# Early stage of a conditioned decoder trunk: five weight places by table, and section weights split by column halves

## The chip, the cores and the metric

The kernel runs on one core of a Trainium2 chip. The time is device microseconds (us) of one execution. The kernel before takes 1154.68 us, the median of three runs (1153.91 to 1155.73). In what follows PE is TensorE, DVE is VectorE, ACT is ScalarE, POOL is GpSimd and SP is SyncE, whose queue issues nearly all of the transfers (DMAs).

## The reference

One layer on 256 tokens of width 1024, all in fp32:

```
mod = silu(c) @ w_ada + b_ada                 # six vectors of 1024: shift, scale, gate, twice
h   = rms_norm(x) * (1 + scale_mix) + shift_mix
z   = h @ w_in                                # 1024 x 7168: sc_x | sc_B | sc_C | u | v | gate_A | gate_B
yA  = sc_B * causal_dwconv3(sc_C * sc_x)
yB  = gelu(u) * (tril(W_s) @ layer_norm(gelu(v)) * ... + b_s)   # ln_v_g is the weight of that norm
x   = x + gate_mix * ((sigmoid(gate_A)*yA + sigmoid(gate_B)*yB) @ w_out)
h   = rms_norm(x) * (1 + scale_ffn) + shift_ffn
x   = x + gate_ffn * moe(h)                   # top 4 of 32 experts, clamped SwiGLU, 12 MiB of weights each
out = rms_norm(x)
```

The spatial product W_s @ v mixes tokens and leaves the channels apart, so the norm's weight, which is one number for each channel, may be put on before the product or after it.

## The kernel before, in words

**Two parts.** The early stage (the adaptive modulation, the projection w_in and the mixer, w_out) reads 28 units of 2 MiB of weights. Then the router orders the experts, and the expert part reads 192 units of 2 MiB, six for each expert, through twelve places in SBUF. Both streams, and a few small tables, are issued one after another by SP, so a transfer whose place isn't free holds back all that are behind it.

**The early units.** The list `units` gives the order. Those called "ada" are slices of w_ada, those called "in" are half a section of w_in (1024 rows by 512 columns; sections are V, then SC_C, SC_X, SC_B, GATE_A, U, GATE_B for the left half of the channels, h = 0, and again for h = 1), and "out" are the halves of w_out. They land in the tile raw, a ring of three places (0, 1, 2), in order of their number. Two early ones go aside, to the tile spare and to slot 7 of the tile W. A unit may be loaded when the one three before it in the ring was used up.

**Split products.** A product in fp32 is made of three passes in a reduced format: ACT copies the weights into wh (`split_high`, L556), DVE subtracts to get wl (`split_low`, L743), and PE makes hh*wh, hl*wh and hh*wl (`product`, L1093). There are two pairs wh, wl in turns, so the weights of section j are split while PE works on section j-1, once it has finished with j-2. Before, each unit is split in two pieces by rows (k), so PE can finish nothing of a section until both pieces are there, and ACT can begin the next unit in that pair only when the whole section is done.

**A section.** PE makes a section in two halves of 256 columns (b = 0, 1), each 48 matmuls of 128x256. I number these halves m = 0 to 23. Behind PE, ACT and DVE take each half out of PSUM and do the convolution, the gates and so on, in the order of an explicit loop over h, section and b. In the same loop DVE splits the section after the next (at b = 1) and works through the adaptive weights of the later four vectors (`weigh`, L790 to L793): each ada unit is multiplied by silu(c) and added into `weighed`, which lies in spare, two passes of 128x2048 a unit, eight units in all. PE sums over the partitions afterwards (`sum_weighed`).

**Spatial product.** In front of the half U, b = 0 PE makes `spatial(2h)` into bank B6, behind U, b = 1 `spatial(2h+1)` into the same bank. The latter waits for `sp_used`: DVE must have taken the former out of B6.

**Going over to the experts.** The first expert units are loaded under waits written by hand: the first when `ada_summed` is 2 (in spare), the second when GATE_B of h = 1 is split, the third when the first half of w_out is split, the fourth when the last section half is done on PE, and so on.

## Time and profile before

| | |
|---|---|
| median of 3 runs | 1154.68 us (1153.91 to 1155.73) |
| profiled execution, span | 1151.8 us (the page gives no other time for it; 2.9 us below the median) |
| PE busy | 957.4 us (83%) |
| DVE, ACT busy | 357.2 us (31%), 243.4 us (21%) |
| moved by DMA | 467.30 MB, mean 406 GB/s |
| last section half on PE | 203.7 us |
| third expert unit issued | 198.23 us |

How to read it: shares are of the whole span, and say little of the first 250 us, where the work is different from the rest. The page's second part cuts the span in 40 slices of 28.8 us. Its first eight slices are the early stage and the router, the rest is the expert part.

### The profile page before, as it was taken

The numbers are of one execution on the slowest core, as the hardware profiler recorded it, in microseconds if no ns is written. First come the engines' busy times: TensorE is split into PE (matmuls) and PEld (weight loads), VectorE is DVE, ScalarE is ACT, GpSimd is POOL, SyncE is SP. The second block draws the span as 40 slices with busy tenths as digits, with TensorE's granted clock in tenths as the row PEclk, the third lists the DMA queues.
The fourth block names the chain that finished last, engine by engine and source line by source line (L and its number), as shares of the span: only waits on it lengthen the run. The fifth ranks groups of instructions, "written<-read, shape, count | busy, mean of one in ns | idle before, by whom it ended". The sixth has DMA issues, their size and how long they took to land.

```text
span 1151.8 us, 23787 instructions
## 1 busy us (share of the span) xinstructions
PE 957.4 (83%) x9707; PEld 505.7 (44%) x9708; DVE 357.2 (31%) x801; ACT 243.4 (21%) x365; POOL 8.6 (1%) x28
## 2 busy tenths in 40 slices
PE   7989999998986976987888888888876876876784
PEld 5789999743442321433333333443321322331331
DVE  3689796571221111212121121221211211211112
ACT  3435444530110110111111111110100100100112
POOL 0010000000000000000000000000000000000000
PEclk9989999999998998999998999999998998898997
DMA  9999788999999999999999999999999999999996
GB/s 358 377 340 357 293 311 318 412 400 428 427 425 427 426 426 427 426 426 425 425 426 427 427 426 426 427 426 427 426 426 426 427 426 427 427 426 426 427 424 273
DMA packets 62413, 467.30 MB, mean 406 GB/s; under 512 B 5180, under 2 KB 6516, under 8 KB 27572
## 3 DMA queue, kind: packets, MB, share of 16 engines
q1 hardware_dynamic: 62144, 466.65, 98.1%
q8 instruction: 19, 0.31, 0.1%
q10 hardware_dynamic: 244, 0.29, 0.1%
q14 instruction: 6, 0.05, 0.0%
HBM read 465.87 MB, written 1.05 MB: 405 GB/s over the span
## 4 chain that ended last, share of the span: by engine, by line
PE 42%; DMA 40%; SPq 8%; DVE 6%; issue 4%; ACT 1%; PEldq 0%; DVEq 0%; ACTq 0%
PE B L1405 22%; DMA trio<-in_w_down_dram 21%; DMA W<-in_w_down_dram 14%; PE B L1093 10%; SPq L411 4%; PE B L1424 3%; DMA W<-in_w_gate_up_dram 3%; SPq L413 3%; PE B L1414 2%; DVE wl L743 2%; DMA spare<-in_w_ada_dram 2%; PE B L1351 2%; PE B L1357 1%; DMA raw<-in_w_in_dram 1%; DVE spare L793 1%
## 5 line engine op out<-in xcount | busy, mean ns | idle before, releaser
L1405 PE MATMUL B<-W,trio 128*32 128x512 f32 (+1 forms) x4784 | 451.4, 522 | 85.6 <-DMA W<-in_w_gate_up_dram 77.3
L1405 PEld LDWEIGHTS B<-W,trio 128*32 128x32 f32 x4784 | 163.3, 112 | 347.7 <-issue 168.2
L661 ACT ACTIVATE EW<-EW 128x256 f32<-128x256 f32 x46 | 19.2, 416 | 683.1 <-DVE EW L1023 683.1
L1023 DVE TENSOR_SCALAR EW<-B 128x256 f32<-128x256 f32 x46 | 19.5, 425 | 463.9 <-PE B L1405 463.9
L1093 PE MATMUL B<-hh,wh 128*128 128x256 f32 x384 | 110.4, 288 | 4.2 <-DVE wl L743 4.2
L1093 PE MATMUL B<-hl,wh 128*128 128x256 f32 x384 | 109.8, 286 | 0.0
L1093 PE MATMUL B<-hh,wl 128*128 128x256 f32 x384 | 109.7, 286 | 0.0
L1414 PE MATMUL B<-b_gu,trio 128*32 128x512 f32 x368 | 50.4, 616 | 66.6 <-issue 55.2
L743 DVE TENSOR_TENSOR wl<-raw,wh 128x2048 fp32r<-128x2048 f32 (+1 forms) x36 | 73.3, 2074 | 18.2 <-ACT wh L556 17.7
L556 ACT ACTIVATE wh<-raw 128x2048 fp32r<-128x2048 f32 (+1 forms) x36 | 60.2, 1719 | 84.0 <-DMA raw<-in_w_in_dram 53.8
L1093 PEld LDWEIGHTS B<-hh,wh 128*128 128x128 f32 x384 | 74.9, 195 | 4.6 <-issue 4.0
L1093 PEld LDWEIGHTS B<-hl,wh 128*128 128x128 f32 x384 | 74.9, 195 | 0.0
L1093 PEld LDWEIGHTS B<-hh,wl 128*128 128x128 f32 x384 | 74.9, 195 | 0.0
L1424 PE MATMUL B<-EW,trio 32*128 32x256 f32 x752 | 67.1, 426 | 8.6 <-PE B L1424 7.8
L1038 DVE TENSOR_TENSOR EW<-B,trio 128x256 f32<-128x256 f32 x46 | 19.5, 425 | 150.4 <-PE B L1405 150.4
L661 ACT ACT_TABLE_LOAD x46 | 59.0, 1283 | 5.8 <-issue 5.0
L1405 PE MATMUL B<-trio 128*32 128x256 f32 x736 | 44.3, 380 | 12.2 <-DMA trio<-in_w_down_dram 12.2
L1351 PE MATMUL B<-HV,trio 128*32 128x256 f32 x752 | 53.7, 400 | 0.2 <-DVE trio L959 0.2
L1405 PE MATMUL B<-spare,trio 128*32 128x512 f32 x368 | 51.7, 678 | 0.0
L1424 PEld LDWEIGHTS B<-EW,trio 32*128 32x128 f32 x752 | 29.4, 182 | 47.7 <-PE B L1424 26.6
L1351 PEld LDWEIGHTS B<-HV,trio 128*32 128x32 f32 x752 | 30.2, 120 | 41.8 <-issue 35.6
L1414 PEld LDWEIGHTS B<-b_gu,trio 128*32 128x32 f32 x368 | 8.6, 107 | 87.8 <-issue 87.8
(245 smaller groups left out, 689.8 us busy)
## 6 DMA issues: line engine op xcount, KB each, us to landing
W<-in_w_gate_up_dram SPq DMA_DIRECT2D x112, 2048.0 KB, 35.2
W<-in_w_down_dram SPq DMA_DIRECT2D x48, 2048.0 KB, 38.4
spare<-in_w_gate_up_dram SPq DMA_DIRECT2D x16, 2048.0 KB, 28.6
trio<-in_w_down_dram SPq DMA_DIRECT2D x15, 2048.0 KB, 41.0
raw<-in_w_in_dram SPq DMA_DIRECT2D x12, 2048.0 KB, 9.5
raw<-in_w_ada_dram SPq DMA_DIRECT2D x9, 2048.0 KB, 9.6
raw<-in_w_in_dram SPq DMA_DIRECT2D x4, 1024.0 KB, 15.7
raw<-in_w_out_dram SPq DMA_DIRECT2D x2, 2048.0 KB, 8.9
```

What stands on the lines that cost most here:

```text
L411: sp.dma_start(unit_pair(u).rearrange("p g n -> p (g n)"), gu_v[e, j]).then_inc(s_unit[u % SLOTS], 16)
L413: sp.dma_start(unit_pair(u), dn_v[e, j - NQ]).then_inc(s_unit[u % SLOTS], 16)
L556: A(part_of(wh[j % 2], c, j), part_of(src, c, j), ACT.Copy).then_inc(split_h, 1)
L661: A(sg, gs, ACT.Sigmoid, scale=ALPHA).then_inc(sig_ready, 1)
L743: V.tensor_tensor(part_of(wl[j % 2], c, j), part_of(src, c, j), part_of(wh[j % 2], c, j).bitcast(f32), ALU.subtract).then_inc(split_l, 1)
L1023: V.tensor_scalar(halves(gs), paired(GU[:, 0:QC]), LIMIT, None, ALU.min).then_inc(gmin_ready, 1)
L1038: V.tensor_tensor(yw, Db[:, 0:QC], gfq, ALU.mult).then_inc(yw_ready, 1)
L1093: t = M(o, left[i], right[j], start=(k == 0 and n == 0), stop=(k == KT - 1 and n == 2))
L1351: t = M(Db[CAP * g:CAP * g + CAP, 0:QC], S[:, a, CAP * g:CAP * g + CAP], HV[:, a, g * QC:(g + 1) * QC], start=(a == 0), stop=(a == TA - 1))
L1405: t = M(o, src[:, k % KQ, CAP * (k // KQ):CAP * (k // KQ) + CAP], w, start=(first and k == 0), stop=(k == KT - 1))
L1414: M(GU[CAP * g:CAP * g + CAP, :], sel[:, g, :], b_gu[:, :], start=True, stop=False)
L1424: M(Yb[a][h][:, (g % 2) * QC:(g % 2) * QC + QC], SwT[rows_, a * P:(a + 1) * P], yw[rows_, :], start=False, stop=True, skip_group_check=Tru ...
```

## The change

- The ring is replaced by a table `homes` that gives each unit its order and one of five places: R0, R1, R2 in raw, the tile spare (which now takes SC_X of h = 0 too) and slot 7 of W (SC_B and GATE_B of h = 0 too). A unit may be loaded when the last one in the same place was used up.
- The section units are split by column halves: piece b holds the columns that half b of the section needs. Piece m + 3 is split in step m, on ACT and on DVE, so the split runs three halves ahead, and a piece waits only for the same half of the section two before.
- `weigh` of the eight units goes to steps m = 1, 4, 7, 8, 12, 14, 17, 19.
- The tables of the mixer (w_spatial, b_spatial, b_ada) are asked for after the ada unit (1, 1), those of the router after GATE_B of h = 0.
- ln_v_g is read as one column per 128 channels with the other small rows, and multiplied in when DVE takes the spatial product out of PSUM (two scalar_tensor_tensor of 128x256 in place of one add of 128x512). The broadcast of it to 128 partitions (512 KiB) and two multiplications of 128x1024 go.
- The first modulation is cut in two around the transposes of x, the router's helper steps (`fhT`, `spread`) move behind the products with w_out.
- The first expert unit now waits for GATE_B's split, the second for `ada_summed`, and the third, as before, for the split of the first half of w_out; but that is now made in two pieces at steps m = 22 and 23, where before the whole of it was made in step m = 21.

```diff
+    homes = [
+        (("ada", 0, 0), R0), (("ada", 0, 1), R1), (("in", V_, 0), R2), (("ada", 0, 2), ASIDE_SPARE), (("ada", 0, 3), ASIDE_M), (("in", V_, 1), R0),
+        (("in", SC_C, 0), R1), (("in", SC_X, 0), ASIDE_SPARE), (("in", SC_B, 0), ASIDE_M), (("ada", 1, 0), R2), (("in", GATE_A, 0), R0), (("ada", 1, 1), R1),
...
+        (("in", SC_B, 1), R2), (("ada", 2, 0), R0), (("in", GATE_A, 1), R1), (("ada", 2, 1), R0), (("ada", 2, 2), R0), (("in", U_, 1), R2),
+        (("in", GATE_B, 1), R1), (("ada", 2, 3), R0), (("out", 0, 0), R2), (("out", 0, 1), R0)]
+    WEIGH_AT = {1: (1, 0), 4: (1, 1), 7: (1, 2), 8: (1, 3), 12: (2, 0), 14: (2, 1), 17: (2, 2), 19: (2, 3)}
...
-            sp.wait_ge(ada_summed, NH)
-            load(0, 0)
             sp.wait_ge(split_l, pieces_before[-3])
+            load(0, 0)
+            sp.wait_ge(ada_summed, NH)
             load(1, 0)
             sp.wait_ge(split_l, pieces_before[-2])
             load(2, 0)
...
-                        if b == 1 and NS * h + n < NS * NH - 1:
-                            split_low(NH + NS * h + n + 2)
+                        m = 2 * (NS * h + n) + b
+                        if 1 <= m < HALVES - 3:
+                            piece_low(m + 3)
+                        if m >= HALVES - 2:
+                            split_low(NH + NS * NH, (b,))
...
+                        if m in WEIGH_AT:
+                            weigh(*WEIGH_AT[m])
...
-                            V.tensor_tensor(stmp.rearrange("p (t a n) -> p t a n", t=2, a=TA),
-                                            B[6][:, :].rearrange("p (t a n) -> p t a n", t=2, a=TA), bias, ALU.add).then_inc(sp_used, 1)
+                            for t in range(2):
+                                k = 4 * h + 2 * b + t
+                                ins = V.scalar_tensor_tensor(gated[:, t], spread_v[:, t], cols[:, 7 * KT + k:7 * KT + k + 1],
+                                                             bs_all[:, k:k + 1, :].broadcast_to([P, TA, P]), ALU.mult, ALU.add)
+                            ins.then_inc(sp_used, 1)
...
-                        if b == 0 and n < 3:
-                            weigh(1 + h, n + 1)
-                        if b == 0 and s == GATE_B and h + 1 < NH:
-                            weigh(2 + h, 0)
...
+                        half_ready(j, b)
                         for tt in range(2):
                             for k in range(KT):
-                                split_ready(j, k)
...
+                    if s == U_ and h == 1:
+                        sum_weighed(2)
```

On DVE, the steps ahead of the first use of the spatial product (bank B6). Before, from the third section's second half on (L743 is a split, L863 the use of B6, L867 what follows it):

```order
L854 TENSOR_TENSOR tmp<-tmp,B5 128x512
L858 TENSOR_TENSOR tmp<-tmp 128x512
L743 TENSOR_TENSOR wl1<-raw,wh1 128x2048 x2
L858 TENSOR_TENSOR tmp<-tmp 128x512
L863 TENSOR_TENSOR tmp<-B6,tmp 128x512
L867 TENSOR_TENSOR tmp<-tmp 128x512
```

And now (L759 is a piece of a split, L808 and L809 are weigh, L892 is the use of B6):

```order
L883 TENSOR_TENSOR tmp<-tmp 128x512
L759 TENSOR_TENSOR wl1<-W,wh1 128x8x256
L808 SCALAR_TENSOR_TENSOR spare<-raw,tmp,spare 128x2048
L809 SCALAR_TENSOR_TENSOR spare<-raw,tmp,spare 128x2048
L883 TENSOR_TENSOR tmp<-tmp 128x512
L759 TENSOR_TENSOR wl1<-W,wh1 128x8x256
L808 SCALAR_TENSOR_TENSOR spare<-raw,tmp,spare 128x2048
L809 SCALAR_TENSOR_TENSOR spare<-raw,tmp,spare 128x2048
L892 SCALAR_TENSOR_TENSOR tmp<-B6,cols,tmp 128x256 x2
L897 TENSOR_TENSOR tmp<-tmp 128x512
```

Two weigh steps, of the ada units (1, 2) and (1, 3), now stand close ahead of the use of B6, the second of them directly with a split piece ahead of it; before, neither stood between GATE_A and B6.

On SP, the early units behind the router's tables (the last row of which is given first). Before:

```order
L405 DMA EW<-in_b_down_dram 32x512 x4
L385 DMA raw<-in_w_ada_dram 128x2x2048
L385 DMA raw<-in_w_in_dram 128x8x512 x3
L385 DMA raw<-in_w_ada_dram 128x2x2048
L385 DMA raw<-in_w_in_dram 128x8x512
L385 DMA raw<-in_w_ada_dram 128x2x2048
L385 DMA raw<-in_w_in_dram 128x8x512
L385 DMA raw<-in_w_ada_dram 128x2x2048
L385 DMA raw<-in_w_in_dram 128x8x512
L385 DMA raw<-in_w_ada_dram 128x2x2048
L385 DMA raw<-in_w_in_dram 128x8x512 x2
L385 DMA raw<-in_w_out_dram 128x8x512 x2
```

And now:

```order
L408 DMA EW<-in_b_down_dram 32x512 x4
L390 DMA raw<-in_w_ada_dram 128x2x2048
L390 DMA raw<-in_w_in_dram 128x8x512
L390 DMA raw<-in_w_ada_dram 128x2x2048
L390 DMA raw<-in_w_in_dram 128x8x512 x2
L390 DMA raw<-in_w_ada_dram 128x2x2048
L390 DMA raw<-in_w_in_dram 128x8x512
L390 DMA raw<-in_w_ada_dram 128x2x2048 x2
L390 DMA raw<-in_w_in_dram 128x8x512 x2
L390 DMA raw<-in_w_ada_dram 128x2x2048
L390 DMA raw<-in_w_out_dram 128x8x512 x2
```

Before, behind the tables stand the ada units (1, 3) and (2, 0) to (2, 3); now (1, 2) and (1, 3), and then the same four, of which (2, 1) and (2, 2) stand together. By the table all four of h = 1 go to one place, R0. The ada unit (1, 3) is now the 17th unit, before it was the 14th.

## Rows read from the trace of the kernel before

**Rows 1.** Page, part 2: DMA share and rate in 40 slices
```profile
DMA  9999788999999999999999999999999999999996
GB/s 358 377 340 357 293 311 318 412 400 428 427 425 427 426 426 427 426 426 425 425 426 427 427 426 426 427 426 427 426 426 426 427 426 427 427 426 426 427 424 273
```

**Rows 2.** Windows: stretch, length, PE clock, DMA share, GB/s
```profile
195.00:198.00 3.00, 1.00 0.12 49
198.00:204.00 6.00, 1.00 0.82 294
204.00:255.00 51.00, 1.00 0.99 403
```

**Rows 3.** Timeline of SP: start, length of issue, third and thirteenth expert unit
```profile
198.23 0.33 SPq L411 DMA_DIRECT2D W<-in_w_gate_up_dram  x1
...
249.98 0.38 SPq L411 DMA_DIRECT2D spare<-in_w_gate_up_dram  x1
```

**Rows 4.** Line L1093 in 50 to 235 us: ns min/median/max, first and last start
```profile
L1093 PE MATMUL B<-hh,wh x384: 277/283/553, 51.6 to 203.5; 128*128 128x256 f32 x192
...
L1093 PE MATMUL B<-hh,wl x384: 278/283/415, 51.9 to 203.7; 128*128 128x256 f32 x192
```

**Rows 5.** Chain that ended last: start, length, what
```profile
119.51 0.89 PE B L1224 x8
120.41 57.59 PE B L1093 x480
178.00 0.99 PE B L1143 x8
```

**Rows 6.** Timeline of PE, first product of the third section
```profile
79.53 0.55 PE L1093 MATMUL B<-hh,wh 128*128 128x256 f32 x1 [3.82 <-DVE wl L743]
```

**Rows 7.** Windows, PE alone: busy, clock, DMA share, GB/s
```profile
76.00:79.50 3.50, 0.00 (x0) 0.85 0.55 158
79.50:85.30 5.80, 5.77 (x27) 0.50 1.08 365
```

**Rows 8.** Timeline of PE, column sums in the second half of V
```profile
38.28 0.96 PE L1131 MATMUL B<-stat,mod 128*128 128x1 f32 x8
```

**Rows 9.** DMA issues of 10.4 us: KB each, us to landing
```profile
W<-in_w_ada_dram SPq DMA_DIRECT2D x1, 2048.0 KB, 23.6
```

**Rows 10.** Windows: PE clock, DMA share, GB/s
```profile
2.00:42.50 40.50, 1.00 1.03 388
...
2.00:106.00 104.00, 0.97 0.99 362
```

**Rows 11.** Timeline of DVE, a section step and a weigh
```profile
81.50 0.68 DVE L844 TENSOR_TENSOR tmp<-tmp,B 128x512 f32<-128x512 f32 x1
82.22 0.35 DVE L849 TENSOR_SCALAR tmp<-tmp,cols 128x256 f32<-128x256 f32 x1
82.61 0.48 DVE L850 SCALAR_TENSOR_TENSOR tmp<-tmp,cols 128x255 f32<-128x255 f32 x1
...
85.07 2.35 DVE L792 SCALAR_TENSOR_TENSOR spare<-raw,tmp,spare 128x2048 f32<-128x2048 f32 x1
```

**Rows 12.** Timeline of DVE, a split and what follows it
```profile
89.85 2.29 DVE L743 TENSOR_TENSOR wl<-raw,wh 128x2048 fp32r<-128x2048 f32 x1
...
94.26 0.68 DVE L844 TENSOR_TENSOR tmp<-tmp,B 128x512 f32<-128x512 f32 x1
```

**Rows 13.** Timeline of ACT, a split and a copy out of PSUM
```profile
75.00 3.71 ACT L556 ACTIVATE wh<-raw 128x2048 fp32r<-128x2048 f32 x2 [6.39 <-DMA raw<-in_w_in_dram]
78.62 0.58 ACT L610 ACTIVATE tmp<-B 128x512 f32<-128x512 f32 x1
```

**Rows 14.** DMA issues of 87.4, 126.2 and 133.1 us, in that order
```profile
raw<-in_w_ada_dram SPq DMA_DIRECT2D x1, 2048.0 KB, 7.6
raw<-in_w_ada_dram SPq DMA_DIRECT2D x1, 2048.0 KB, 8.6
raw<-in_w_in_dram SPq DMA_DIRECT2D x1, 2048.0 KB, 8.0
```

**Rows 15.** Chain that ended last, in the first expert rounds
```profile
260.52 1.57 issue
...
263.16 6.87 PE B L1405 x64
...
276.96 2.08 issue
...
280.21 8.45 PE B L1405 x64
```

More of the change, by code:

```diff
@@ L76, in hybrid_trunk @@
     unit_no = {u: n for n, u in enumerate(units)}
+    in_order = [("in", V_, h) for h in range(NH)] + [("in", s, h) for h in range(NH) for s in SECTIONS] + [("out", 0, h) for h in range(NH)]
+    assert [units[n] for n in split_units] == in_order
     NU = len(units)
@@ L174, in hybrid_trunk @@
         id_row, more_row, unit_row, upto, passed, hit_round, round_row = [order_row(6 + i) for i in range(7)]
-        rank_col, id_col, more_col, owner, expert_col, place_rank = [stat[:, 51 + i:52 + i] for i in range(6)]
+        rank_col, id_col, more_col, owner, expert_col = [stat[:, 51 + i:52 + i] for i in range(5)]
         rounds = mod[0:1, 1, 0:6 * E + 1].bitcast(i32)
@@ L308, in act_bank, with home, in_section, product_done @@
             return act_order.index((h, s, b)) + 1
-        ASIDE = (3, 4)
-        aside_at = (spare[:, :], slot(7))
-        def place(n):
-            return n if n < ASIDE[0] else n - len(ASIDE)
+        def home(n):
+            return homes[n][1]
         def raw_slot(n):
-            if n in ASIDE:
-                return aside_at[ASIDE.index(n)]
-            return raw[:, (place(n) % RING) * UW:(place(n) % RING + 1) * UW]
+            if home(n) == ASIDE_SPARE:
+                return spare[:, :]
+            if home(n) == ASIDE_M:
+                return slot(7)
+            return raw[:, home(n) * UW:(home(n) + 1) * UW]
         def landed(n):
-            if n in ASIDE:
-                return s_aside[ASIDE.index(n)], 16
-            return s_slot[place(n) % RING], 16 * (place(n) // RING + 1)
-        def product_done(eng, j):
+            return s_slot[home(n)], 16 * len([m for m in range(n + 1) if home(m) == home(n)])
+        def in_section(j):
+            return NH <= j < NH + NH * NS
+        def product_done(eng, j, c):
             if j == 0:
@@ L356, in _ @@
             for n, (kind, s, h) in enumerate(units):
-                if n not in ASIDE and place(n) >= RING:
-                    m = next(o for o in range(n) if o not in ASIDE and place(o) == place(n) - RING)
+                before_it = [m for m in range(n) if home(m) == home(n)]
+                if before_it:
+                    m = before_it[-1]
                     if m in ada_units:
@@ L796, in weigh, with piece_low @@
                     dve.nop().then_inc(weighed_ready, 1)
-            split_low(2)
-            weigh(1, 0)
-            split_low(3)
+            def piece_low(t):
+                split_low(NH + t // 2, (t % 2,))
+            piece_low(0)
+            piece_low(1)
             dve.wait_ge(v_gelu, TA * NH)
@@ L1103, in _, with modulation @@
             keep_warm(WARM_FIRST, B[5])
-            pe.wait_ge(s_rows, 64)
-            TR(B[6][:, 0:7 * KT], rows, ident[0:7 * KT, 0:7 * KT]).then_inc(rowsT_done, 1)
-            def modulation(part, g):
+            pe.wait_ge(s_rows, 80)
+            TR(B[6][:, 0:8 * KT], rows, ident[0:8 * KT, 0:8 * KT]).then_inc(rowsT_done, 1)
+            def modulation(part, g, ks=range(KT)):
                 if part + g == 0:
@@ L1113, in modulation @@
                 n = unit_no[("ada", 0, 2 * part + g)]
-                if part == 0 and g == 1:
+                if part == 0 and g == 1 and ks[0] == 0:
                     pe.wait_ge(s_ada_top, 16)
@@ L1118, in modulation @@
                 w = raw_slot(n).rearrange("p (k n) -> p k n", k=KT)
-                for k in range(KT):
+                for k in ks:
                     j = k % 4
-                    if part == 0 and g == 1 and k == 4:
-                        arrived(n)
                     t = M(first_bank(part, g)[32 * j:32 * j + 32, :], cond[:, k, :], w[:, k, :], start=(k < 4), stop=(k >= 4))
-                t.then_inc(ada_used, 1)
+                if ks[-1] == KT - 1:
+                    t.then_inc(ada_used, 1)
             def turn_sums(part, g):
@@ L1146, in _ @@
             modulation(0, 0)
+            modulation(0, 1, range(0, 4))
             pe.wait_ge(xn_ready, TA)
@@ L1152, in _ @@
             t.then_inc(xnT_done, 1)
+            modulation(0, 1, range(4, KT))
             turn_sums(0, 0)
-            modulation(0, 1)
             turn_sums(0, 1)
@@ L1190, in _ @@
             v_low(0)
+            v_high(2)
             modulation(1, 0)
-            v_high(2)
+            v_high(3)
             turn_sums(1, 0)
-            v_high(3)
             modulation(1, 1)
@@ L1250, in _ @@
                         t.then_inc(sec_done, 1)
-                    if s == SC_X and h == 0:
+                        if s == GATE_B and h == 0 and b == 0:
+                            sum_weighed(1)
+                    if s == SC_B and h == 0:
                         turn_spatial()
```

138 lines of the change are left out of this document (70 added, 68 removed).

## The prediction, made blind

> **What bounds the kernel now.** I read the page's slices first [rows 1]: from the ninth slice on the DMAs move 425 to 428 GB/s and never pause. The expert part is bound by its stream of weights, so the end comes when the last byte has come, and any change early is worth only what it moves that stream. Windows around the going over [rows 2] and the issues in it [rows 3] show where the stream begins: the DMAs are nearly idle at 195 to 198 us (49 GB/s), because the third expert unit is issued only at 198.23 us. Behind that there are small gaps only: 204 to 255 us run at 403 GB/s, so (427-403)/427 x 51 = 2.9 us are lost there, and nothing later. So two quantities decide: when the third expert unit is issued (call it L), and how much of the 2.9 us goes.
>
> L hangs on PE's early stage. The section products run from 51.6 to 203.7 us [rows 4] on the chain, at 57.59/480 = 0.12 us a matmul [rows 5], so 5.76 us for a half section of 48. All 24 halves are 138.2 us, what lies between them 6.6: turning the spatial weights 1.0 (as long as the sums), four spatial products of 0.9, two sums of 1.0 [rows 5]. PE left alone would end at 51.6 + 138.2 + 6.6 = 196.4. The missing 7.3 us are one stall, 3.82 us at 75.7 us, for DVE's split [rows 6], behind which PE ran 5.8 us at half clock (27 matmuls in 5.77 us, where 48 fit: 2.5 us lost) [rows 7], and about 1 us at 108.
>
> **What the change takes away.** The split three halves ahead takes away that stall: the piece for the half at 75 us is made by about 65 us. That is 7.3 us on PE. Moving v_high up and cutting the first modulation lets the fourth modulation unit be used when it lands, at 10.4 + 23.6 = 34.0 us [rows 9], where its column sums ended a row of work at 38.28 us [rows 8]: sums at 37.1 instead, so 1.2 us. The broadcast norm weight and its two passes go, which shortens DVE by 2.5 us where it has rests, and the DMA by 0.5 MB. Without new waits the last section half ends at 203.7 - 7.3 - 1.2 = 195.2 us. The new extra DMA on ACT's queue costs nothing: PE's first modulation waits for w_ada anyway. The router's helper steps that move behind w_out shorten the way there by some 1 to 2 us, hidden behind the stream, which by then has a backlog.
>
> **What it adds, first place.** DVE works in order, and in step m = 8 it now does weigh of ada unit (1, 3) ahead of taking the spatial product out of B6, and PE's spatial(1) waits for that. The ada unit is the 17th. Up to it 35 MiB of units and 2.35 MiB of tables must land, 39.2 MB. The places come free early enough that the DMA hardly pauses until then. At the rate of the first 40 us, 388 GB/s, that is 101 us, with the start at 2 and 2 us to the landing signal 105 us; at the mean of 2 to 106 us, 362 GB/s, which holds before's pauses (one at 76 us) and its slow small tables, 112 us [rows 7, 10]. I take 107.6: the pauses go, the tables stay. DVE is ready for it at about 105 (splits of 2.2, half of 94.26-89.85; weighs of 4.8, 89.85-85.07; convolution steps of 3.6, 85.07-81.50 [rows 11, 12]; without rest from 54 us on). Weigh 4.8 and two steps of 0.5 [rows 11]: B6 is free at 113.5. PE is there at 50.4 + 10 x 5.76 + 1.0 + 0.9 = 109.9. So PE stands still 3.6 us (0.8 if the unit lands by 105; 8 if at 112). The stall of 3.82 us cost 2.5 us of half clock behind it [rows 6, 7], I charge the same here.
>
> **Second place.** In h = 1 all four ada units go to R0, so each is asked for only when DVE has used the one before, and each trip is bare: a 2 MiB unit into idle DMAs takes 7.6, 8.6 and 8.0 us from issue to landing [rows 14]; I take 8.1. From the end of PE's half m = 11 (t = 0): sigmoid and two DVE steps 2.0, ACT piece 1.9 (half of 3.71 [rows 13]) to 2.5, DVE piece 4.7, two steps 6.1, weigh (2, 0) 9.8; trip 17.9; weigh (2, 1) 22.7; trip of (2, 2) with U right behind it 8.1 + 5.4 = 36.2; ACT and DVE piece of U 40.3; weigh (2, 2) 45.1; trip 53.2; weigh (2, 3) 58.0; step, piece, B6 taken 62.0. PE reaches spatial(3) at 10 x 5.76 + 0.9 = 58.5. A second stall of 3.5 us (2.0 with trips of 7.6). For the clock the rows are of two minds: after 1.57 us of rest a stream of 64 matmuls took 6.87 us, after 2.08 us 8.45 [rows 15]. I charge 0.8, half of that difference.
>
> By the Trainium skill ("DMA: Bandwidth & Descriptors", section on the anatomy of one DMA) a transfer costs about 2.0 us and its bytes at 436 GB/s. That would be 6.8 us for such a trip; the trace doesn't agree, its least is 7.6. By that rule the second stall would shrink by three times 1.3 us and go, and the time would be some 4.3 us less than I forecast.
>
> **Third place.** The third expert unit now waits for the second piece of w_out's first half, made in step m = 23: it needs the sigmoid behind half m = 22 (0.6), ACT's piece (1.9), DVE's (2.2): L = T - 5.76 + 4.7 = T - 1.0, where T is the end of the last half. Before it was T - 5.5. So 4.5 us of what PE gains don't reach the stream. The first two units (issued at about T - 15 and T - 12) hide in time, 2 x 4.9 us. Against this all waits behind L come closer together than the units take: fourth at T, then T + 4, T + 10, T + 12, T + 24, T + 36, thirteenth at about T + 45 (249.98 before [rows 3]), while ten units take 49 us. So I count 2.8 of the 2.9 us as won.
>
> **The sum.** T = 109.9 + 3.6 (stall) + 0.9 + 5.8 + 1.0 + 5.8 + 2.5 (clock) + 58.5 + 3.5 (stall) + 0.9 + 1.0 + 11.5 + 0.8 (clock) = 205.7. L = 204.7, 6.5 us later than before; 6.5 - 2.8 = +3.7 us. The profiled execution would go from 1151.8 to 1155.5; it lies 2.9 us under the median of the runs, so I forecast 1158.4 us.
>
> **Rivals.**
> - R1, only the second stall, a small first one (the 17th unit lands by 105.5 us, 0.8 to 1.3 us of rest, which the 1.57 us row says costs no clock) and no clock loss at the second: T = 195.2 + 1 + 3 = 199.2, L = 198.2 as before, gain 2.8: 1151.9. For it: the table loads are asked for later and half a MB less. Against: the mean rate of before.
> - R2, no stall at all, short trips (the rule of the page cited above, and 7.6 us in one row) and early landings: T = 195.2, L 4.0 us earlier than before, and 2.8: 1147.9. This is what the change seems made for; against it, four bare trips in a row on one place.
> - R3, faster not, slower more: the 17th unit lands at 110 to 112, the first stall is 6 to 8 us; it decides from a landing after 109 us on. The price is 1 us for 1 us: 1161 to 1163.
> - R4, in between: one stall costs its clock, the other doesn't: 1155.5.
> - The change not doing what it says (PE still waits for a split at a section's start) would show as a wait on L759 near 75 us; the order speaks against it.
>
> **How the numbers follow.** A change within 0.2% (1152.4 to 1157.0) can't be told from none here. Forecast (both stalls, at least one half clock, 1156 to 1160.5) 0.42; R1 (1150.5 to 1154) 0.25; R4 0.15; R3 0.10; R2 0.08. Faster: R2 and somewhat over half of R1, 0.22. Same: the rest of R1, R4 and a sixth of the forecast, 0.32. Slower 0.46. The range goes from the middle of R1's low side, 1150.5, to R3's near end, 1162. The likeliest case alone: 1156 to 1160.5.
>
> **What would show it.** In the profile after: no PE wait before the section at 75 us; PE waiting on DVE (the use of B6) near 110 us and near 188 us; DVE waiting for an ada unit in front of L808 near 105 us and three times behind 135 us; granted clock 0.5 behind the first stall; the third expert unit 1 us ahead of the last section half; 426 GB/s without gaps from there. I am wrong if PE's sections end before 200 us, or if the third expert unit isn't what begins the unbroken stream.

## The result, and the profile after

The changed kernel takes 1163.35 us (median of four runs, 1161.47 to 1164.12), the kernel before in the same session 1154.40 (four runs). The ratio is 1.0074, with a 95% interval of 1.0058 to 1.0089: slower, by more than twice what I forecast, and outside my range, which ended at 1162. The spans of the profiled executions are 1159.7 and 1151.8 us, 7.9 apart, where my sum had 3.7. That is 4.2 us of the miss; the other 0.8 is that this profiled span lies 3.7 us under its median, where I had put 2.9.

The windows of the kernel after come first. Each line gives the stretch, its length, the busy time of PE, its weight load, DVE, ACT and POOL (in brackets the number of instructions), and, as in [rows 2], PE's granted clock, the DMAs' busy share and their GB/s.

```profile
120.00:200.00 80.00, 75.33 (x613) 72.52 (x612) 60.44 (x51) 28.66 (x23) 0.00 (x0) 0.98 0.70 260
204.00:255.00 51.00, 49.40 (x281) 35.36 (x283) 36.60 (x94) 20.40 (x37) 1.72 (x10) 0.93 0.96 398
212.00:262.00 50.00, 48.27 (x302) 30.72 (x300) 33.31 (x97) 18.80 (x36) 1.72 (x10) 0.93 1.01 423
```

From 120 to 200 us the DMAs move 260 GB/s. The same window of the kernel before:

```profile
120.00:200.00 80.00, 80.00 (x669) 79.03 (x667) 66.98 (x54) 35.93 (x29) 0.00 (x0) 1.00 0.82 304
```

44 GB/s less over 80 us is 3.5 MB, and at 427 GB/s that is 8.2 us: nearly the whole loss arises in this one window (from 0 to 120 us the changed kernel moves 361 GB/s against 358, from 200 to 262 us 401 against 405). Behind its third expert unit the stream then runs without a break, 423 GB/s from 212 to 262 us. Next the issues on SP's queue at the going over, of after (start, duration, line, destination):

```profile
188.90 0.37 SPq L390 DMA_DIRECT2D raw<-in_w_out_dram  x1
196.53 0.35 SPq L414 DMA_DIRECT2D spare<-in_w_gate_up_dram  x1
207.20 1.33 SPq L414 DMA_DIRECT2D W<-in_w_gate_up_dram  x2
256.73 0.37 SPq L414 DMA_DIRECT2D W<-in_w_gate_up_dram  x1
```

The third expert unit, L, is issued at 207.20, 9.0 us after that of before [rows 3], the thirteenth at 256.73 (249.98 before, [rows 3]). The two stalls of PE, and what DVE and ACT wait for ahead of them (in brackets the idle time and its releaser):

```profile
114.23 2.08 PE L1249 MATMUL B<-tmp,HV 128*128 128x128 f32 x8 [2.60 <-DVE tmp L892]
192.76 2.08 PE L1249 MATMUL B<-tmp,HV 128*128 128x128 f32 x8 [4.67 <-DVE tmp L892]
```
```profile
108.35 2.35 DVE L808 SCALAR_TENSOR_TENSOR spare<-raw,tmp,spare 128x2048 f32<-128x2048 f32 x1 [2.55 <-DMA raw<-in_w_ada_dram]
169.42 2.29 DVE L759 TENSOR_TENSOR wl<-raw,wh 128x2048 fp32r<-128x2048 f32 x1 [3.96 <-ACT wh L560]
171.63 2.35 DVE L808 SCALAR_TENSOR_TENSOR spare<-raw,tmp,spare 128x2048 f32<-128x2048 f32 x1
184.13 2.35 DVE L808 SCALAR_TENSOR_TENSOR spare<-raw,tmp,spare 128x2048 f32<-128x2048 f32 x1 [1.92 <-DMA raw<-in_w_ada_dram]
```
```profile
167.40 3.72 ACT L560 ACTIVATE wh<-raw 128x2048 fp32r<-128x2048 f32 x2 [12.74 <-DMA raw<-in_w_in_dram]
```

Both stalls stand at the uses of B6, as forecast, and no stall is left where [rows 6] had one. The second begins far ahead of PE: ACT rests 12.7 us for the unit of U, DVE waits behind it, and weigh (2, 2) is made only at 171.6, though its unit was asked for at 153.2 and had landed at 162.0. Now the granted clock of after, in windows (22 to 26 us, around the two stalls, and in the stretch of the router). It is given as a share: 1.00 is the higher of its two levels, 2.4 GHz, 0.50 the lower, 1.2 GHz, and a value between is the mean of a window that had both:

```profile
22.00:26.00 4.00, 3.84 (x10) 3.08 (x11) 4.00 (x7) 4.00 (x7) 0.00 (x0) 0.57 1.05 386
112.00:116.00 4.00, 1.77 (x9) 1.77 (x9) 3.72 (x5) 3.34 (x3) 0.00 (x0) 0.77 0.55 157
116.00:120.00 4.00, 4.00 (x30) 4.00 (x30) 3.93 (x5) 0.00 (x0) 0.00 (x0) 0.80 1.05 402
192.70:202.50 9.80, 9.74 (x67) 8.10 (x68) 4.56 (x6) 0.06 (x1) 0.00 (x0) 0.83 1.04 424
236.00:240.00 4.00, 3.22 (x23) 2.68 (x26) 1.93 (x4) 0.60 (x1) 0.00 (x0) 0.63 1.00 422
240.00:244.00 4.00, 4.00 (x19) 2.65 (x12) 2.09 (x10) 1.67 (x2) 0.89 (x4) 0.52 0.99 422
```

Two of these falls I had not forecast: in the head, and at 236 to 244 us. There is a third at the very end. In the chain that ended last, the last transfer of weights and the last two products of eight matmuls, before and then after:

```profile
1101.94 38.12 DMA trio<-in_w_down_dram
1142.03 0.83 PE B L1424 x8
1142.91 0.79 PE B L1424 x8
```
```profile
1109.14 37.65 DMA trio<-in_w_down_dram
1148.85 1.35 PE B L1446 x8
1150.25 1.31 PE B L1446 x8
```
```profile
1148.00:1152.00 4.00, 2.47 (x16) 1.03 (x16) 0.71 (x2) 0.44 (x1) 0.00 (x0) 0.55 0.00 0
```

The weights are all there at 1140.1 us before and at 1146.8 after, 6.7 us later. The two products behind them took 1.62 us before and 2.66 after, under a granted clock of 0.55. So of the 7.9 us between the spans the stream of weights explains 6.7 and the clock in the last products 1.0.

### The profile page after: what moved, and what is told of

Read it like the earlier page. It is cut to its first block, busy times and chain, and to the rows that moved or that the text cites. A ratio compares the mean times of both kernels' runs of the same rounds, so it can differ in the third digit from the quotient of the medians.

```text
span 1159.7 us, 23804 instructions
## 1 busy us (share of the span) xinstructions
PE 961.5 (83%) x9707; PEld 509.4 (44%) x9708; DVE 356.1 (31%) x802; ACT 243.5 (21%) x366; POOL 7.2 (1%) x28
## 4 chain that ended last, share of the span: by engine, by line
DMA 42%; PE 40%; SPq 7%; DVE 6%; issue 4%; ACT 1%; PEldq 0%; DVEq 0%; ACTq 0%
PE B L1427 22%; DMA trio<-in_w_down_dram 18%; DMA W<-in_w_down_dram 13%; DMA W<-in_w_gate_up_dram 6%; SPq L414 4%; PE B L1118 4%; DMA raw<-in_w_ada_dram 4%; PE B L1446 3%; PE B L1436 2%; PE B L1373 2%; SPq L416 2%; PE B L1196 1%; DVE spare L809 1%; DVE wl L759 1%; DMA raw<-in_w_in_dram 1%
## 5 line engine op out<-in xcount | busy, mean ns | idle before, releaser
L1427 PE MATMUL B<-W,trio 128*32 128x512 f32 (+1 forms) x4784 | 457.7, 524 | 83.3 <-DMA W<-in_w_gate_up_dram 66.1
L1436 PE MATMUL B<-b_gu,trio 128*32 128x512 f32 x368 | 50.7, 620 | 66.8 <-issue 55.3
L759 DVE TENSOR_TENSOR wl<-raw,wh 128x2048 fp32r<-128x2048 f32 (+1 forms) x30 | 59.8, 2005 | 8.2 <-ACT wh L560 7.7
L560 ACT ACTIVATE wh<-raw 128x2048 fp32r<-128x2048 f32 (+1 forms) x30 | 49.9, 1684 | 54.3 <-DMA raw<-in_w_in_dram 37.3
L1446 PEld LDWEIGHTS B<-EW,trio 32*128 32x128 f32 x752 | 30.2, 188 | 48.8 <-PE B L1446 27.2
L1427 PE MATMUL B<-spare,trio 128*32 128x512 f32 x368 | 45.8, 609 | 4.3 <-DMA spare<-in_w_gate_up_dram 4.3
```

The costliest lines, as they stand in the source:

```text
L560: A(part_of(wh[j % 2], c, j), part_of(src, c, j), ACT.Copy).then_inc(split_h, 1)
L759: V.tensor_tensor(part_of(wl[j % 2], c, j), part_of(src, c, j), part_of(wh[j % 2], c, j).bitcast(f32), ALU.subtract).then_inc(split_l, 1)
L1427: t = M(o, src[:, k % KQ, CAP * (k // KQ):CAP * (k // KQ) + CAP], w, start=(first and k == 0), stop=(k == KT - 1))
L1436: M(GU[CAP * g:CAP * g + CAP, :], sel[:, g, :], b_gu[:, :], start=True, stop=False)
L1446: M(Yb[a][h][:, (g % 2) * QC:(g % 2) * QC + QC], SwT[rows_, a * P:(a + 1) * P], yw[rows_, :], start=False, stop=True, skip_group_check=Tru ...
```

## The experiments

Each is an edit of the changed kernel unless it says otherwise. T is the end of the last section half; the time given is the median of the runs, the ratio is to the kernel before on the same chip.

**e1: w_out's first half split whole in step 22.**

```diff
-                        if m >= HALVES - 2:
-                            split_low(NH + NS * NH, (b,))
+                        if m == HALVES - 2:
+                            split_low(NH + NS * NH, (0, 1))
```
(and the same for split_high)

> The changed kernel with one thing undone: both pieces of w_out's first half are split in step m = 22, ahead of the gate, instead of one in step 22 and one in 23. Theory (the unbroken stream of expert weights begins with the third expert unit, and its issue sits behind that second piece): the unit is issued 6 to 7 us ahead of PE's last section half instead of 1 us, PE's own end stays at 207.9 us, and the kernel takes 4 to 5 us less than the changed one (1163.35), about 1158.5. Rival (the loss is the later end of PE's sections alone, the stream would catch up): less than 1 us.

1161.8 us, ratio 1.0058 [1.0041, 1.0075]. The issues and the window behind them:

```profile
201.31 0.33 SPq L414 DMA_DIRECT2D W<-in_w_gate_up_dram  x1
256.88 0.38 SPq L414 DMA_DIRECT2D W<-in_w_gate_up_dram  x1
```
```profile
208.00:262.00 54.00, 52.31 (x320) 34.09 (x318) 35.61 (x100) 21.12 (x38) 1.72 (x10) 0.94 0.96 398
```

I had expected 1158.5. L moved 5.9 us forward, the time 1.5, and the intervals of the two ratios overlap. What L gave was given back behind it: 208 to 262 us run at 398 GB/s, where the changed kernel has 416, and the DMAs come near to a stop ahead of the thirteenth unit (104 GB/s at 255 to 258 us). The thirteenth unit waits for the first places that the expert part gives free, and came no earlier. So L isn't the one thing that sets the end.

**e2: weigh (2, 3) behind the taking of B6, in step 20.**

```diff
-... 17: (2, 2), 19: (2, 3)}
+... 17: (2, 2)}
...
+                        if m == 20:
+                            weigh(2, 3)
```

> The changed kernel, with the weigh of ada unit (2, 3) moved from step 19 to behind the taking of B6 in step 20. Theory (PE's second stall comes from a weigh that waits for its unit in front of the taking of B6): the wait of 4.67 us at 192.8 us and the slow clock behind it go, PE's last section half ends about 6 us sooner (near 202), the third expert unit is issued as much sooner, and the kernel takes 5 to 6 us less than the changed one, about 1158. Rival (DVE is late there anyway, by the whole chain of trips to R0): PE then waits at the column sums for the same weigh, and under 1 us is won.

1160.89 us, ratio 1.0050 [1.0034, 1.0067], where I had expected 1158 and T near 202. The stall at the second B6 is gone, but PE waits 2.44 us at the column sums for that same weigh; T is 204.9. The wait moved to its next reader and shrank.

```profile
190.88 1.06 PE L1169 MATMUL B<-spare,tmp 128*32 128x512 f32 x8 [2.44 <-DVEq L812]
```

**e3: weigh (1, 3) in step 9.**

```diff
-    WEIGH_AT = {..., 8: (1, 3), ...
+    WEIGH_AT = {..., 9: (1, 3), ...
```

> The changed kernel, with the weigh of ada unit (1, 3) in step 9 instead of 8, so behind the first taking of B6. Theory: PE's first stall (2.6 us at 114.2 us) and the slow clock behind it (1.8 us) go; the steps of h = 1 hang on PE's end of step 11 and come sooner with it, so the last section half ends 4 to 5 us sooner and the kernel takes 4 to 5 us less, about 1159. Rival (the chain of trips in h = 1 hangs on when the DMA delivers, not on PE): the first stall goes but the second grows by as much, and nothing is won.

1154.43 us (ten runs), ratio 0.9994 [0.9985, 1.0004]: 9 us better than the changed kernel, by one number. DVE takes B6 and only then does the weigh:

```profile
106.29 0.87 DVE L892 SCALAR_TENSOR_TENSOR tmp<-B,cols,tmp 128x256 f32<-128x256 f32 x2
110.13 2.35 DVE L808 SCALAR_TENSOR_TENSOR spare<-raw,tmp,spare 128x2048 f32<-128x2048 f32 x1
```
```profile
22.00:26.00 4.00, 4.00 (x20) 3.26 (x19) 4.00 (x7) 3.45 (x5) 0.00 (x0) 1.00 1.05 388
112.00:116.00 4.00, 4.00 (x36) 4.00 (x35) 3.72 (x5) 1.41 (x2) 0.00 (x0) 1.00 0.46 158
```

I had expected 1159. The first stall and the fall of the clock behind it are gone (4.3 us: 2.60 of rest, and a fifth of 8.5 us); the second stall stays, 4.42 us, and T is 202.2. What more was won comes, in this profiled execution, from places ahead of the edit and behind it: the clock was 1.00 in the head (1.9 us), in the router's stretch, and in the last two products (1.0 us). Whether that belongs to this kernel or to this execution isn't shown. It can't be all chance of executions: all ten times of e3 (1154.05 to 1155.86) lie more than 5 us under all five of the changed kernel (1161.02 to 1164.12).

**e4: PE's order in the first 40 us as before.**

```diff
             modulation(0, 0)
-            modulation(0, 1, range(0, 4))
             pe.wait_ge(xn_ready, TA)
...
-            v_high(2)
             modulation(1, 0)
-            v_high(3)
+            v_high(2)
             turn_sums(1, 0)
+            v_high(3)
```
(modulation (0, 1) whole behind turn_sums (0, 0), as before)

> The changed kernel with PE's order in the first 40 us as before: the second modulation in one piece behind the transposes of x, and the third modulation ahead of the third step of V. In the changed kernel PE's sections begin at 52.1 us, before at 51.6, where I had forecast 50.4. Theory (a product of V at half clock stands in front of the modulation whose weights have landed): sections begin at 51.6 or sooner, and since ada unit (1, 3) lands when the DMA brings it, PE only waits longer for it: 0 to 0.5 us won. Rival (the beginning passes on to the end one to one): the kernel takes 0.5 to 1.5 us less.

1162.55 us, ratio 1.0068 [1.0051, 1.0085]; not to be told from the changed kernel. T is 207.3. The head's clock was 1.00 in this execution, and the sections still begin only at 51.6, as before; with the new order and the clock at 1.00 they begin at 50.2 to 50.7 (e3, e5, e7, e10 to e12). So the new order is worth 0.9 to 1.4 us at the start of the sections, as I had reckoned (1.2).

**e5: the edits of e1, e2 and e3 together.**

> The changed kernel with three edits at once: weigh (1, 3) in step 9 in place of 8, weigh (2, 3) behind the taking of B6 in step 20, and both pieces of w_out's first half split in step 22. Theory of two bounds (the end follows the later of: the third expert unit's issue L, against 198.23 and less the 2.9 us of gaps; the thirteenth unit's issue, against 249.98): from the run with weigh (1, 3) alone, which had T (last section half) at 202.2 with a stall of 4.4 us and some 1.9 us of half clock at the second place, T becomes 196 to 198.3 (the column sums may wait up to 2.4 us), L = T - 6.4 = about 191.5, thirteenth unit at T + 46.7 = about 244.5. The first bound says 9.6 us earlier, the second 5.5; the second decides: about 5.3 us faster than before, some 1149.5 to 1150.5. Rival, L alone decides: 9.6 us faster, 1146. Rival, nothing is left to win since the first two units hold the stream: 1153.

1154.32 us (ten runs), ratio 0.9991 [0.9982, 1.0001]. No better than e3 alone, though L is 9.5 us earlier:

```profile
185.60 0.37 SPq L390 DMA_DIRECT2D raw<-in_w_out_dram  x1
191.95 0.33 SPq L414 DMA_DIRECT2D W<-in_w_gate_up_dram  x1
249.99 0.37 SPq L414 DMA_DIRECT2D W<-in_w_gate_up_dram  x1
```

The thirteenth unit stands where before has it. "L alone" (1146) is out, and so is the 1149.5 to 1150.5 that I took for likely. T is 199.8, where I had expected 196 to 198.3 (PE waits 2.63 us at the column sums), and the thirteenth unit comes at T + 50.2 and not at T + 46.7, behind a router stretch in which the granted clock is 0.50 from 228 to 236 us.

**e7: the router's helper steps (turning of the shift row, spreads, turn_x) back between the products with w_out, and the copy of the shift row back from ACT to DVE.**

```diff
+                    if h == 0 and ks[0] == 0:
+                        ...
+                            t = TR(B[6][:, P * q:P * q + P], mod[:, 1, P * q:P * q + P], ident[:, :])
+                        t.then_inc(fhT_done, 1)
+                    if h == NH - 1 and ks[0] == 0:
+                        ...
+                            turn_x(0, a)
...
-            for a in range(TA):
-                turn_x(0, a)
```

> The changed kernel with the router's helper steps (turning of the shift row, the three spreads, turn_x(0, a)) put back between the products with w_out, where they were before, and the copy to shm back on DVE. The early stage is untouched: T 207.9, L 206.9 as in the changed kernel. Theory M (the moved steps are what made the way from T to the first release of round 0 longer and gave the half clock at 236 to 244 us): round 0 at T + 42.0 = 249.9, thirteenth unit at T + 46.3 = 254.2 where the changed kernel has 256.7, granted clock 1.0 at 236 to 244: 2.5 us less, about 1160.9. Theory C (the clock falls there for another reason, from what PE did long before or by chance from run to run; the moved steps are innocent): thirteenth unit at T + 48.8, same time as the changed kernel within 0.1%: 1163.

1162.52 us, ratio 1.0060 [1.0043, 1.0077]. I had expected 1160.9. The first stall was longer in this execution (the ada unit (1, 3) was there only at 110.0), so T is 210.5, but the stretch behind T is as expected of the moved steps: thirteenth unit at 256.69, T + 46.2, with the clock at 1.00.

```profile
115.92 2.08 PE L1250 MATMUL B<-tmp,HV 128*128 128x128 f32 x8 [5.87 <-DVE tmp L890]
```
```profile
236.00:240.00 4.00, 4.00 (x35) 2.85 (x33) 3.73 (x8) 1.52 (x5) 0.00 (x0) 1.00 1.05 442
240.00:244.00 4.00, 3.06 (x21) 1.91 (x21) 3.79 (x13) 2.37 (x5) 0.91 (x5) 1.00 0.97 410
```

Over all runs: with the helper steps in their old places (before, e7, e8, e10, e11, e12) the clock was 1.00 in this stretch six times of six; with them moved (after, e1 to e5, e9, e13) it fell in seven of eight (not in e3), to 0.50 to 0.53 in its lowest window, and sooner where T is sooner. The time hardly changed, since here L decides.

**e8: the kernel before, with w_out's first half split in steps 22 and 23.**

```diff
-                        if b == 1 and NS * h + n < NS * NH - 1:
+                        if b == 1 and NS * h + n < NS * NH - 2:
                             split_low(NH + NS * h + n + 2)
+                        if NS * h + n == NS * NH - 1:
+                            split_low(NH + NS * NH, (b,))
```

> The kernel before with only the third place: the first half of w_out is split in two pieces in steps m = 22 and 23, where it was split whole in m = 21. T stays at 203.7, L goes from 198.23 to T - 1.0 = 202.7, 4.5 us later. Theory of two bounds: the thirteenth unit stays at 249.98 (the router's path doesn't change), the gaps behind L take up 2.9 us, so 1.6 us slower than before, ratio 1.001 to 1.002. Rival A, L counts in full: 4.5 us slower, 1.004. Rival B, L counts for nothing as long as the thirteenth unit comes at its time: no change, 1.000.

1156.11 us (ten runs), ratio 1.0011 [1.0002, 1.0021]. L is 203.31, 5.1 us later, and the time 1.5 later (the span 2.6). The DMAs stand still from 196 to 204 us, and yet half of these 5.1 us are covered, since the thirteenth unit, which has moved by 0.3 us only, had left that much slack. It is the rest that [rows 2] show at 195 to 198 us, made longer.

```profile
196.00:200.00 4.00, 4.00 (x36) 4.00 (x35) 2.00 (x3) 1.44 (x2) 0.00 (x0) 1.00 0.01 4
200.00:204.00 4.00, 4.00 (x35) 4.00 (x34) 3.51 (x3) 1.48 (x2) 0.00 (x0) 1.00 0.00 0
```

**e9: the changed kernel once more, for a second profile.**

> The changed kernel once more, unchanged, for a second profile. If the falls of the granted clock in the head (22 to 26 us) and in the router's stretch (236 to 244 us) belong to the program, they stand in this profile at the same places and the column sums end at 38.7, T at 207.9, thirteenth unit at T + 48.8. If they are chance from one execution to the next, one or both are gone, with first section half at 50.2 in place of 52.1 and the thirteenth unit at T + 46.5.

1161.02 us, span 1159.2. Both falls of the clock stand again (0.58 at 22 to 26 us, 0.52 at 240 to 244), the stalls are 2.87 and 4.48 us, the thirteenth unit 256.61. The head's fall isn't in every kernel, though. Of those with the same instructions up to there, e3, e5, e7, e10, e11 and e12 had 1.00 at 22 to 26 us, and sections that start at 50.2 to 50.7 in place of 52.1; e1 (0.58), e2 (0.66) and e13 (0.70) had the fall too, with sections from 52.1, 51.4 and 51.2.

**e10: e5 with the helper steps of e7.**

> The kernel with the three early edits (weigh (1, 3) in step 9, weigh (2, 3) behind B6's taking in step 20, w_out's first half split in step 22) and the router's helper steps back in their old places. Theory (the thirteenth unit, asked for when round 0 of the expert part gives its places free, sets the end, and the moved helper steps cost it about 4 us by half clock at 228 to 244 us): T 199.8 and L about 192 as with the three edits alone; clock 1.0 from 216 to 256; round 0 at T + 42 = 241.8, thirteenth unit at T + 46.2 = 246.0, where it stood at 249.99: 4 us less than the three edits alone, 2.5 to 4 us faster than before: 1151 to 1152. Rival: another thing than the thirteenth unit holds the end at the time of before (the bound is in the stream): no difference to the three edits, 1154.3. Rival: the clock falls all the same: 1154 to 1155.

1153.81 us (eleven runs), ratio 0.9990 [0.9980, 1.0000], where I had expected 1151 to 1152; 0.5 us under e5: nothing that can be told apart.

```profile
185.15 0.37 SPq L390 DMA_DIRECT2D raw<-in_w_out_dram  x1
191.50 0.33 SPq L414 DMA_DIRECT2D W<-in_w_gate_up_dram  x1
244.04 0.38 SPq L414 DMA_DIRECT2D W<-in_w_gate_up_dram  x1
```

Now the thirteenth unit is 6 us early and L nearly 7, and still only 1 us of the span is won. So a third place holds the stream: the second half of w_out, issued at 185.15, with both first expert units right behind it. Before, it was issued at 177.42. It lands in R0, and waits there for the last of four ada units that go through R0 one after another.

**e11: e10 with weigh (2, 3) in step 19 again.**

> The same kernel as the last, but with weigh (2, 3) in step 19 as in the changed kernel. The second stall returns: some 4.4 us of PE's rest and 1 to 2 us of half clock against 2.6 us of rest at the column sums; T 202.2, thirteenth unit at T + 46.2 = 248.4, L 195.8. By the thirteenth unit's bound 1.6 us before that of the kernel before, so 0.5 to 1.5 us faster: 1153.5 to 1154. Theory of L alone: L 195.8 - 2.9 is 5.3 us earlier, so 1149 to 1150.

1153.01 us (eleven runs), ratio 0.9987 [0.9978, 0.9996]. T is 4.0 us later than in e10 (201.8 and 197.8), L 3.1, and the time is the same: a later T and a later L cost nothing here, while out (0, 1), asked for 2.75 us sooner (182.40 and 185.15), may have paid for them.

**e12: e11 with weigh (2, 2) in step 16.** In e10 DVE stood idle for 4.0 us ahead of weigh (2, 2), which waited behind the piece of U for a unit that was asked for after its own:

```profile
163.24 2.29 DVE L757 TENSOR_TENSOR wl<-raw,wh 128x2048 fp32r<-128x2048 f32 x1 [4.01 <-ACT wh L560]
```

```diff
-... 14: (2, 1), 17: (2, 2), 19: (2, 3)}
+... 14: (2, 1), 16: (2, 2), 19: (2, 3)}
```

> The changed kernel with weigh (1, 3) in step 9, weigh (2, 2) in step 16 in place of 17, w_out's first half split whole in step 22, and the router's helper steps in their old places; weigh (2, 3) stays in step 19. In the run with weigh (2, 3) in step 20 DVE did weigh (2, 2) only at 165.5 us, behind the piece of U, whose unit landed at 161; the last ada unit was asked for at 170.2, and out (0, 1) and the first two expert units, queued behind it, at 185.2 to 186.5. Theory D (what counts is from when the DMA has work without a break, with the bytes still to come; the chain of ada units through the one place R0 sets that): weigh (2, 2) at 158.6, ada (2, 3) asked for at 163.4 and landed at 171.5, used up by about 178.5 in step 19 without a wait; out (0, 1) asked for at 178.5, the first expert unit right behind; no second stall, T = 195.3, thirteenth unit 241.4: 5 to 6.5 us less than the 1153.8 of that run: 1147.5 to 1149. Theory L (the third expert unit's issue, T - 6.4 = 188.9 against 191.5, is what counts): 2.6 us less, 1151. Theory N (the end doesn't follow the early stage any more, since two runs with L at 191.5 and 194.6 gave the same time): 1153 to 1154.

1145.79 us (five runs), ratio 0.9930 [0.9916, 0.9944]: the fastest of all, 7.2 us under e11 by one number (6.6 by the ratios), and 1.7 us under the 1147.5 to 1149 that I had expected. The issues, and DVE's weigh steps:

```profile
163.71 0.37 SPq L390 DMA_DIRECT2D raw<-in_w_ada_dram  x1
177.99 0.37 SPq L390 DMA_DIRECT2D raw<-in_w_out_dram  x1
189.73 0.33 SPq L414 DMA_DIRECT2D W<-in_w_gate_up_dram  x1
241.85 0.37 SPq L414 DMA_DIRECT2D W<-in_w_gate_up_dram  x1
```
```profile
158.95 2.35 DVE L806 SCALAR_TENSOR_TENSOR spare<-raw,tmp,spare 128x2048 f32<-128x2048 f32 x1
173.22 2.35 DVE L806 SCALAR_TENSOR_TENSOR spare<-raw,tmp,spare 128x2048 f32<-128x2048 f32 x1 [0.76 <-DMA raw<-in_w_ada_dram]
```
```profile
120.00:200.00 80.00, 80.00 (x651) 78.32 (x651) 65.39 (x57) 31.88 (x27) 0.00 (x0) 1.00 0.85 329
```

Weigh (2, 2) is made 12.7 us earlier than in the changed kernel, so its place, the next trip and the end of the chain are earlier, PE has no stall in its sections (80.00 of 80 us busy), and the DMAs run at 329 GB/s where they had 260.

**e13: the changed kernel with two numbers changed.**

```diff
-... 8: (1, 3), 12: (2, 0), 14: (2, 1), 17: (2, 2), ...
+... 9: (1, 3), 12: (2, 0), 14: (2, 1), 16: (2, 2), ...
```

> The changed kernel with two numbers of WEIGH_AT changed and nothing else: weigh (1, 3) in step 9 in place of 8, weigh (2, 2) in step 16 in place of 17. No first and no second stall: T = 195.3 (or 1 to 2 us more where the clock falls in the head). L = T - 1.0 = 194.3, 3.9 us earlier than before; out (0, 1) asked for at about 178.5, so the first two expert units have landed before L and the DMA rests until it; from L on unbroken. The router's stretch at half clock again: thirteenth unit at T + 48.8 to 50 = 244 to 245, 5 to 6 us earlier than before. Theory D and theory L agree here: stream 3.9 us and some 1.5 us of the gaps earlier, 1149.5 to 1150.5. If the second stall needs more than this one step (the ada unit (2, 3) lands later than 173): T 198 and 1152 to 1153.

1147.70 us (five runs), ratio 0.9940 [0.9926, 0.9953]. I had expected 1149.5 to 1150.5. T is 196.0, with no stall in the sections; out (0, 1) at 178.41, L at 195.35, thirteenth unit 244.63. These two numbers are 15.7 us: the 9.0 that the change lost, and 6.7 more that it had to give.

**One reckoning for all runs.** A unit takes 2.097 MB / 427 GB/s = 4.9 us of the stream. Each issue that waits for a release bounds the stream. To compare them I bring them all to the place of the third expert unit. L stands as it is. The thirteenth unit has ten units ahead of it, the third to the twelfth, so 49.1 us are taken off. Between the issue of out (0, 1) and the third lie three units, itself and the first two expert units, so 14.7 us are added. The largest of the three, against 200.9 of before, should be how much later the stream ends. The end of the last product that waits for weights (1141.2 us before) shows how much later it did; the next column is what the two products of eight behind it took beyond the 1.62 us of before, and the last the difference of the spans (1151.8 before):

| kernel | out (0, 1) + 14.7 | L | 13th - 49.1 | largest - 200.9 | last weights' product - 1141.2 | two products - 1.62 | span - 1151.8 |
|---|---|---|---|---|---|---|---|
| before | 192.1 | 198.2 | 200.9 | 0 | 0 | 0 | 0 |
| after | 203.6 | 207.2 | 207.6 | +6.7 | +6.7 | +1.0 | +7.9 |
| e1 | 203.8 | 201.3 | 207.8 | +6.9 | +6.4 | +1.0 | +7.5 |
| e2 | 205.4 | 204.2 | 206.0 | +5.1 | +4.8 | 0 | +5.0 |
| e3 | 197.0 | 201.5 | 199.8 | +0.6 | +0.3 | 0 | +0.4 |
| e4 | 203.0 | 206.6 | 206.8 | +5.9 | +6.2 | 0 | +6.3 |
| e5 | 200.3 | 192.0 | 200.9 | 0 | +0.3 | +0.9 | +1.2 |
| e7 | 205.7 | 209.8 | 207.6 | +8.9 | +9.1 | +0.7 | +9.8 |
| e8 | 192.4 | 203.3 | 201.2 | +2.4 | +2.6 | 0 | +2.6 |
| e9 | 203.5 | 207.1 | 207.5 | +6.6 | +6.3 | +1.0 | +7.4 |
| e10 | 199.9 | 191.5 | 194.9 | -1.0 | -1.0 | 0 | -1.0 |
| e11 | 197.1 | 194.6 | 198.9 | -2.0 | -1.1 | 0 | -0.9 |
| e12 | 192.7 | 189.7 | 192.8 | -8.1 | -7.2 | +1.0 | -6.1 |
| e13 | 193.1 | 195.4 | 195.5 | -5.4 | -5.7 | 0 | -5.7 |

It gives the end of the stream within 0.5 us, for e11 and e12 within 0.9; the span is that and the two products, within 0.2. It was made after the runs, except for its column of out (0, 1) in e12, which was expected before that run, and it was not tried on a kernel that it was not made from. Spans are of one execution each. Where two of the three columns lie within half a us of each other (after, e4, e9, e12 and e13) the table doesn't say which of them held the stream.

## Why the prediction was wrong

The direction was right, and so was what the forecast says stops PE: both stalls stand where it put them, the third expert unit is issued 0.7 us ahead of T, and the stream behind it has no break. What failed is sizes in the sum, and one term that I put at nothing. In the order of its steps:

- **The stall at 75 us goes:** right. **Start of the sections at 50.4:** 52.1 here (52.0 in e9), by the clock's fall at 22 to 26 us; in the runs without the fall 50.2 to 50.7, so the step was right where the clock holds. I had taken the head's clock for whole: 1.7 us.
- **First stall 3.6 us and 2.5 of clock:** 2.60, with the ada unit landing at 108.3 (forecast 107.6); PE came later by the head's 1.7. Behind it the clock was 0.80 on the mean of 114.2 to 122.7 us, all of it ahead of 120, some 1.7 us, and not at 0.50 throughout as I had forecast. Together 4.3 against 6.1: 1.8 us too much, which by luck takes back the head's 1.7. e3 shows the mechanism alone.
- **Second stall 3.5 us and 0.8 of clock: this is the term of the sum that failed.** It took 4.67, and the clock was 0.83 over 9.8 us, 1.7 us. Together 6.4 against 4.3, 2.1 us too little. The 0.8 was half of a difference between two rows of other work [rows 15]. The three trips of this chain took 9.2, 8.8 and 7.7 us from issue to landing, where I took 8.1, and the unit of U, behind one of them, 13.8 where I took 13.5. On the path to the stall the first trip was 1.1 us longer than I took it, U landed 0.7 us later behind the second's issue (14.2 against 13.5), and the third was 0.4 shorter: 1.4 us, of which 1.2 stand in the stall. None of the three was as bare as I had taken it: the unit issued at 134.40 landed only 3.0 us into the first, U went out 0.4 us behind the second, and w_out's first unit 3.1 us behind the third. The issues of the three (KB each, us from issue to landing):

```profile
raw<-in_w_ada_dram SPq DMA_DIRECT2D x1, 2048.0 KB, 9.2
raw<-in_w_ada_dram SPq DMA_DIRECT2D x1, 2048.0 KB, 8.8
raw<-in_w_ada_dram SPq DMA_DIRECT2D x1, 2048.0 KB, 7.7
```

- By the Trainium skill ("DMA: Bandwidth & Descriptors", section on the anatomy of one DMA) such a trip would be 6.8 us, an estimate from a fit that the section gives for transfers issued by GpSimd; these are issued by SP. This kernel's three trips don't agree; their least is 7.7.
- **T = 205.7:** 207.9. **L = T - 1.0:** 207.20 = T - 0.7. So L is 9.0 us later than before, not 6.5: 2.5 us of the miss.
- **2.8 of the 2.9 us of gaps are won:** the stream ends 6.7 us later where L is 9.0 later, so 2.3 were won: 0.5 us of the miss. By the table the thirteenth unit, at T + 48.8 where I took T + 45, is level with L here. I had counted the moved helper steps as 1 to 2 us less; e7 and e9 show that with them the clock falls in the router's stretch and the thirteenth unit comes 2.6 us later behind T. That costs this kernel at most 0.4 us, since L is as late.
- **"The end comes when the last byte has come":** the stretch behind the last weights isn't always of one length. The two last products took 1.0 us more than before, under a clock of 0.55, and 0.2 us more lies in this stretch and in rounding: 1.2 us of the miss. The forecast has nothing for it.
- 3.7 + 2.5 + 0.5 + 1.2 = 7.9, the measured difference of the spans; 0.8 more lies between span and median.
- **"Two quantities decide":** L and the gaps did for this kernel. As a general statement it was wrong: e5, e10 and e11 moved L by 12.6 to 15.7 us against the changed kernel and stopped at the time of before, by the table on the thirteenth unit (e5 and e11) or on the chain through R0 (e10). My own list of the second place had that chain, step by step, with weigh (2, 2) behind the piece of U; I used it for PE's stall alone and not for the DMAs' rest, which was worth more.
- **Rivals:** R1 and R2 needed short trips and an early landing; they were wrong in that. R2's price was right: e13, the changed kernel with no stall, took 1147.70 where R2 had 1147.9, but it comes from the order of the weigh steps. R3, a first stall of 6 to 8 us from a landing at 110 to 112, is what e7's execution nearly shows (5.87 us, landing by 110.0, 1163.48), by the same early stage; but the 1163.4 of the changed kernel came another way.

That the helper steps cause the fall in the router's stretch is shown by e7 against the changed kernel and by the counts of runs; by what mechanism was not tried. Why the clock falls in the head (5 profiles of 11 with the same instructions up to there) and in the last products is open: each kernel but the changed one has one profile, so a chance of the execution can't be told from something in the program.

## What to carry to other kernels

When a stream of weights is the bound, don't ask which issue starts it: for each issue that waits for a release, take its time less the transfer time of what can run ahead of it, and the latest of these sets the end (here within 0.9 us in thirteen profiles against that of before). An edit that moves any other is worth little, as e1, e5 and e10 show. And where several units go through one place in turns, the step that uses each up belongs as early in its engine's order as the unit lands, ahead of anything that waits for a later transfer: one number in a table was worth 7 us, two 16 (e12, e13).

## What the runs showed of the hardware

PE's granted clock fell to 0.52 in the router's stretch at 240 to 244 us while PE was busy 4.00 of 4 us, and in the four us ahead of it (0.63) PE was busy 3.22. In the kernel before and in all kernels with the helper steps in their old places it stayed at 1.00 there, with PE busy 3.06 of 4 us in e7 at 240 to 244. The clock of a stretch can't be read from that stretch's busy share alone; what came ahead of it counts, as e7 shows, where only the order of the work was changed, and one small copy moved from ACT to DVE.

A rest of PE cost clock behind it in each of these rows: after 2.60 us the granted clock was 0.80 at 116 to 120 us (after), after 4.67 us 0.83 over 9.8 us (after), after 5.87 us 0.50 at 116 to 120 us (e7). A fall in the head (0.57, 0.58, 0.58, 0.66 and 0.70 at 22 to 26 us in after, e9, e1, e2 and e13, 1.00 in six others with the same instructions up to there) goes with sections that start 0.5 to 1.9 us later. And the two last products of eight matmuls took 1.62 us in eight profiles and 2.28 to 2.66 in six (after, e1, e5, e7, e9 and e12), which was 0.7 to 1.0 us of the span.

The three 2 MiB transfers of the second stall's chain, each with one other unit under way for a part of its time, took 7.7 to 9.2 us from issue to landing (three of before took 7.6 to 8.6, [rows 14]).
